# Crossing the second chunk of each pair over TensorE's array, and spreading the key products and turns through the inverse of an RWKV-7 recurrence

## The reference

```
def _wkv7_step(state, inp):
    r_t, w_t, k_t, v_t, a_t, b_t = inp
    sa = einsum('bhvk,bhk->bhv', state, a_t)
    state = state * w_t[:, :, None, :] + sa[..., None] * b_t[:, :, None, :] + v_t[..., None] * k_t[:, :, None, :]
    y = einsum('bhvk,bhk->bhv', state, r_t)
    return state, y
```

## Time and profile before

| | us |
|---|---|
| median of three runs | 2360.57 |
| the profiled execution | 2356.65 |
| its span | 2354.9 |
| the recurrence, from its first matmul to the first of the next stage | 897.69 to 1137.29 in the span |
| TensorE busy in the span | 2167.8 (92%) |
| VectorE busy in the span | 1294.9 (55%) |

### The profile page before, as it was taken

One profiled execution on the slowest core, in us unless ns is written; L12 is line 12 of the kernel. 1 busy time (PEld: TensorE's weight loads), 2 busy tenths in 40 slices (PEclk: granted clock), 3 DMA queues, 4 the chain that ended last, 5 costly groups with the idle time before them and its releaser, 6 DMA issues. The chain is left out here.

```text
span 2354.9 us, 36913 instructions
## 1 busy us (share of the span) xinstructions
PE 2167.8 (92%) x16050; PEld 1654.4 (70%) x16050; DVE 1294.9 (55%) x1837; ACT 768.9 (33%) x1111; POOL 281.4 (12%) x188
## 2 busy tenths in 40 slices
PE   7998989999979957999898999999976988999998
PEld 3885767887858617999455888887534665888885
DVE  2335756665454566555435766733386536766534
ACT  2434644443224430000224222322244624222322
POOL 0000003335400071111320000000004400000000
PEclk9998999999989968999979999999887999999999
DMA  6232002212213200000111233232320021333231
GB/s 270 96 99 82 1 10 84 69 56 80 95 60 99 83 0 3 4 4 4 32 33 56 90 99 99 90 99 80 104 69 1 1 63 54 99 99 99 90 99 45
DMA packets 46850, 158.81 MB, mean 67 GB/s; under 512 B 5232, under 2 KB 7280, under 8 KB 46688
## 3 DMA queue, kind: packets, MB, share of 16 engines
q1 hardware_dynamic: 44832, 150.84, 20.0%
q10 hardware_dynamic: 1856, 5.60, 0.7%
HBM read 154.28 MB, written 2.14 MB: 66 GB/s over the span
## 5 line engine op out<-in xcount | busy, mean ns | idle before, releaser
L923 PE MATMUL banks<-up_x_high,up_w_high 128*128 128x512 f32 x1056 | 412.3, 390 | 8.5 <-DVE up_w_low L917 3.9
L924 PE MATMUL banks<-up_x_low,up_w_high 128*128 128x512 f32 x1056 | 411.5, 390 | 0.0
L925 PE MATMUL banks<-up_x_high,up_w_low 128*128 128x512 f32 x1056 | 411.4, 390 | 0.0
L917 DVE TENSOR_TENSOR up_w_low<-weight_ring,up_w_high 128x1024 fp32r<-128x1024 f32 x132 | 161.6, 1226 | 272.1 <-ACT up_w_high L912 272.1
L912 ACT CAST up_w_high<-weight_ring 128x1024 fp32r<-128x1024 f32 x132 | 138.3, 1049 | 365.4 <-PE banks L925 340.8
L923 PEld LDWEIGHTS banks<-up_x_high,up_w_high 128*128 128x128 f32 x1056 | 198.5, 188 | 53.8 <-issue 11.7
L925 PEld LDWEIGHTS banks<-up_x_high,up_w_low 128*128 128x128 f32 x1056 | 198.6, 188 | 41.2
L924 PEld LDWEIGHTS banks<-up_x_low,up_w_high 128*128 128x128 f32 x1056 | 198.7, 188 | 41.0
L1443 POOL TENSOR_TENSOR hproj_w_low<-weight_ring,hproj_w_high 128x1024 fp32r<-128x1024 f32 x43 | 106.0, 2465 | 510.4 <-ACT hproj_w_high L1251 510.4
L976 DVE SCALAR_TENSOR_TENSOR act<-banks,cols,act 128x511 f32<-128x511 f32 (+1 forms) x176 | 131.9, 749 | 6.2
L1131 PE MATMUL banks<-hproj_x_high,hproj_w_high 128*128 128x512 f32 x224 | 90.1, 402 | 5.2 <-DVE hproj_x_low L1396 3.4
(11 more groups left out here) (453 smaller groups left out, 4391.3 us busy)
## 6 DMA issues: line engine op xcount, KB each, us to landing
weight_ring<-in_up SPq DMA_DIRECT2D x88, 512.0 KB, 3.6
weight_ring<-in_down SPq DMA_DIRECT2D x44, 512.0 KB, 3.6
weight_ring<-in_w_ada SPq DMA_DIRECT2D x24, 512.0 KB, 5.7
weight_ring<-in_w_rkv SPq DMA_DIRECT2D x24, 512.0 KB, 3.3
weight_ring<-in_w_in SPq DMA_DIRECT2D x20, 512.0 KB, 3.4
weight_ring<-in_w_out SPq DMA_DIRECT2D x16, 512.0 KB, 3.3
weight_ring<-in_w_q SPq DMA_DIRECT2D x8, 512.0 KB, 6.3
weight_ring<-in_w_k SPq DMA_DIRECT2D x8, 512.0 KB, 3.3
```

What stands on the lines that cost most here:

```text
L917: nc.vector.tensor_tensor(w_low[:, n % 2, :], ring[:, i % RING, :], w_high[:, n % 2, :].bitcast(f32), ALU.subtract).then_inc(wl_made, 1)
L923: nc.tensor.matmul(PS[:, bank, :], high, x_high[:, k, :], start=start, stop=False)
L924: nc.tensor.matmul(PS[:, bank, :], high, x_low[:, k, :], start=False, stop=False)
L925: return nc.tensor.matmul(PS[:, bank, :], low, x_high[:, k, :], start=False, stop=stop)
```

## The change

`SIDES` gives chunk x = 0 the same half in and out (`SAME`) and chunk x = 1 the other half out (`CROSS`), in `q_level`, in the product that adds to G, and in `make_w`. With this the second chunk's Q, GT and W lie with the two heads of each pair swapped, and its products of these kinds use the upper right and lower left corners. `q_level` and the product for G are written with the chunks alternating inside `p`, so that four products to four corners follow one another. The product for GT is written chunk by chunk, after that for G, and reads and writes one half. DVE takes both G before both GT. POOL's last step of the second chunk is cut in two, one for each half, so a pair has 7 operations there and not 6. The products of k and the turns leave `all_grams`: they follow half levels of the same pair (`fill`), the k products of the first chunk behind the first `q_level`, those of the second chunk in two parts, and one turn behind each half level from the fifth on. The banks move accordingly.

```
+                def key_gram(i, x, part):
+                    c = 2 * i + x
+                    if part == 0:
+                        pe.wait_ge(gram_moved, 6 * i + 3 + 2 * x)
+                    for p in range(4 * part, 4 * part + 4):
...
+                def fill(i, h):
+                    if h == 0:
+                        key_gram(i, 0, 0)
+                        key_gram(i, 0, 1)
+                    elif h in (2, 3):
+                        key_gram(i, 1, h - 2)
+                    elif h >= 4:
+                        turn(2 * i + (h - 4) // 3, (h - 4) % 3, (v, kt, bt)[(h - 4) % 3])
 
                 def q_level(i, l):
                     for x in range(2):
                         if l == 1:
-                            pe.wait_ge(start_made, 6 * i + 3 * x + 3)
-                            pe.wait_ge(gram_moved, 6 * i + 5 + x)
+                            pe.wait_ge(start_made, 7 * i + 1 + 3 * x)
+                            pe.wait_ge(gram_moved, 6 * i + 4)
                         else:
                             pe.wait_ge(g_moved, 8 * i + 2 * (l - 2) + x + 1)
...
+                    for p in range(8):
+                        for x in range(2):
+                            nt = with_b[(2 * i + x) % 4].rearrange("p (h w) -> p h w", h=8)
+                            for half, side in SIDES[x]:
+                                mm = nc.tensor.matmul(PS[side, x, pair_cols(p)], nt[half, p, 0:LC], G_[x][half, pair_cols(p)], start=True, stop=True)
...
                 def g_level(i, l):
                     for x in range(2):
                         pe.wait_ge(q_moved, 10 * i + 2 * (l - 1) + x + 1)
                         if l > 1:
                             pe.wait_ge(gt_moved, 10 * i + 2 * (l - 2) + x + 1)
+                    if l == 1:
+                        pe.wait_ge(start_made, 7 * i + 7)
+                    if l < LEVELS:
                         for p in range(8):
+                            for x in range(2):
+                                c = 2 * i + x
+                                for half, side in SIDES[x]:
+                                    mm = nc.tensor.matmul(PS[half, x, pair_cols(p)], GT_[c % 4][side, pair_cols(p)], Q_[x][side, pair_cols(p)], start=True, stop=True)
+                    for x in range(2):
+                        c = 2 * i + x
+                        for p in range(8):
+                            for half, side in SIDES[x]:
+                                mm = nc.tensor.matmul(PS[side, 2 + x, pair_cols(p)], Q_[x][side, pair_cols(p)], GT_[c % 4][side, pair_cols(p)], start=True, stop=True)
                         mm.then_inc(g_made, 1)
```

More of the change, by code:

```diff
@@ L1701, in program @@
         HALVES = (slice(0, HD), slice(HD, P))
+        SAME, CROSS = tuple(zip(HALVES, HALVES)), tuple(zip(HALVES, HALVES[::-1]))
+        SIDES = (SAME, CROSS)
         by_pair = lambda t: t.rearrange("p (h l) -> p h l", h=8)
@@ L1733, in turn @@
                         for half in HALVES:
-                            mm = nc.tensor.matmul(PS[half, 6 + i % 2, pair_cols(p)], of_head(t, p, half, c), ident64[half, :], start=True, stop=True)
+                            mm = nc.tensor.matmul(PS[half, 4 + i % 2, pair_cols(p)], of_head(t, p, half, c), ident64[half, :], start=True, stop=True)
                     mm.then_inc(turned, 1)
@@ L1744, in all_grams @@
                     gram(b, 2, bt, (at_, rt))
[L1745 to L1754, removed]
+                def key_gram(i, x, part):
[3 more added lines that the diff above has]
+                    for p in range(4 * part, 4 * part + 4):
+                        for j, right in enumerate((at_, rt)):
+                            at0 = 2 * p + j
+                            for half in HALVES:
+                                mm = nc.tensor.matmul(PS[half, 4 + at0 // 8, at0 % 8 * LC:(at0 % 8 + 1) * LC], of_head(kt, p, half, c), of_head(right, p, half, c), start=True, stop=True)
+                    if part == 1:
+                        mm.then_inc(grams, 1)
+                def fill(i, h):
[6 more added lines that the diff above has]
+                        turn(2 * i + (h - 4) // 3, (h - 4) % 3, (v, kt, bt)[(h - 4) % 3])
                 def q_level(i, l):
@@ L1765, in q_level @@
[L1765 to L1768, removed]
+                    for p in range(8):
[3 more added lines that the diff above has]
+                                mm = nc.tensor.matmul(PS[side, x, pair_cols(p)], nt[half, p, 0:LC], G_[x][half, pair_cols(p)], start=True, stop=True)
+                            if p == 7:
+                                mm.then_inc(q_made, 1)
@@ L1778, in g_level @@
+                    if l < LEVELS:
                         for p in range(8):
[L1779 to L1784, removed]
+                            for x in range(2):
+                                c = 2 * i + x
+                                for half, side in SIDES[x]:
+                                    mm = nc.tensor.matmul(PS[half, x, pair_cols(p)], GT_[c % 4][side, pair_cols(p)], Q_[x][side, pair_cols(p)], start=True, stop=True)
+                                if p == 7:
+                                    mm.then_inc(gn_made, 1)
@@ L1792, in make_w @@
                         pe.wait_ge(s_zero, 1)
-                    pe.wait_ge(turned_moved, min(6 * (c // 2 + 2), 24))
+                    pe.wait_ge(turned_moved, 6 * (c // 2 + 1))
                     ak = with_k[c % 4].rearrange("p (h w) -> p h w", h=8)
                     for p in range(8):
[L1796 to L1799, removed]
+                        for half, side in SIDES[c % 2]:
+                            nc.tensor.matmul(PS[side, 6, pair_cols(p)], of_head(at_, p, half, c), S_[half, pair_cols(p)], start=True, stop=False)
+                        for half, side in SIDES[c % 2]:
+                            mm = nc.tensor.matmul(PS[side, 6, pair_cols(p)], ak[half, p, 0:LC], of_head(v, p, half, c), start=False, stop=True)
                     mm.then_inc(w_made, 1)
@@ L1805, in make_u @@
                     for p in range(8):
-                        for half in HALVES:
-                            mm = nc.tensor.matmul(PS[half, 7, pair_cols(p)], GT_[c % 4][half, pair_cols(p)], W_[half, pair_cols(p)], start=True, stop=True)
+                        for half, side in SIDES[c % 2]:
+                            mm = nc.tensor.matmul(PS[half, 7, pair_cols(p)], GT_[c % 4][side, pair_cols(p)], W_[side, pair_cols(p)], start=True, stop=True)
                     mm.then_inc(u_made, 1)
@@ L1844, in _ @@
                         for part in range(2):
+                            step = 2 * (l - 1) + part
                             if i < NCH // 2:
                                 (g_level if part else q_level)(i, l)
-                            step = 2 * (l - 1) + part
+                                fill(i, step)
                             if i and step < 8:
@@ L1905, in _ @@
                     if i < NCH // 2:
-                        for n, x in enumerate((0, 0, 1, 1, 0, 1)):
+                        for n, x in enumerate((0, 0, 1, 1)):
                             take_gram(i, n, x)
@@ L1910, in _ @@
                             if i < NCH // 2:
-                                for x in range(2):
-                                    (take_g if part else take_q)(i, l, x)
+                                for take in (take_g, take_gt) if part else (take_q,):
+                                    for x in range(2):
+                                        take(i, l, x)
                             step = 2 * (l - 1) + part
+                            if i < NCH // 2 and step in (0, 3):
+                                take_gram(i, 4 + step // 3, step // 3)
                             if i and step < 8:
@@ L1940, in _ @@
                 for i in range(NCH // 2 + 1):
[L1941 to L1946, removed]
+                    for step in range(2 * LEVELS):
+                        if i < NCH // 2 and step >= 4:
+                            take_turned(2 * i + (step - 4) // 3, (step - 4) % 3)
+                        if i and step in (2, 6):
+                            take_y(2 * i - 2 + step // 4)
         checkpoint("wkv", ALL(r))
```

50 lines of the change are left out of this document (29 added, 21 removed).

## The result

The changed kernel is slower: a median of 2367.12 us against 2358.86 us of the kernel before in the same rounds (20 runs each), ratio 1.0032, 95% interval 1.0023 to 1.0042. Forecast were 2343 us, a range of 2334 to 2362 and a chance of 0.81 for faster.

What follows compares the result with a forecast made beforehand. TensorE's order of instructions was taken to bound the state recurrence stage. Terms: -33.6 + 10.5 + 1.0 + 4.2 + 4.0 - 6.9 + 3.4 = -17.4 us, giving 2343 us against the median; range 2334 to 2362.

Steps and rivals of the forecast that it cites:

- the sum of the other terms: State recurrence stage: all waits added and removed plus clock losses, without the four-corner saving; +16.2 us.
- the wait on POOL: Before `q_level` 1, behind the 96 grams: TensorE waits for POOL's fourth operation, four pairs, 10.5 us in all.
- half levels on DVE: Before `g_level`, TensorE waits while DVE masks both Q: 7 times 0.6 us, 4.2 us.
- grams on ACT: The grams of three pairs wait for ACT's last turned copy: 0.9 us each, 2.7 us.
- the last carry's turns: The first step of the last carry waits for its turns: 0.8 us.
- an assumed two: Clock falls behind the four new 2.5 to 2.7 us waits: two assumed, 1.7 us lost each, 3.4 us.
- the first pair's second wait on POOL: First pair's `g_level` 1 waits for POOL's three further operations: 1.0 us.
- I take the whole of it: 1152 matmuls of `q_level` and the product for G fall from 58.3 to 29.2 ns on four corners: -33.6 us.
- the issue floor: Rival, 6%: TensorE takes one small record in 22 ns, 44 ns a four-corner matmul; saving shrinks 17.0 us, 2360 us.
- the text's own point, 44 ns: Break-even: from 44 ns for a four-corner matmul on, the saving no longer pays the other 16.2 us.
- the pace also halves with the clock: Check on 64-column matmuls, 58.3 against 106 ns: issue at a fixed rate would not halve, so the array sets pace.
- two corners at a time: Rival, 9%: corners sharing rows or columns take turns, 58.3 ns a matmul stay; +16.2 us, 2377 us, slower.

Runs made afterwards that it cites:

- the two-corner run: Changed kernel with both chunks on the same side of the array (SAME for x = 0 and x = 1), all else as changed: 2377.46 us, ratio 1.0071.
- the wide products: Half level products at 128 moving columns, half as many: changed kernel 2336.83 us; same on two corners 2368.34 us; stages 30.3 us apart.
- half_before: Kernel before, every state recurrence product cut to 32 weight and 32 moving columns, same instructions: 2344.39 us, ratio 0.9934.
- pool_first: Changed kernel with GpSimd's two operations adding the identity to G moved first in each pair: 2362.86 us, ratio 1.0025.

## Why the prediction was wrong

**Right:** the array's speed in four corners, and the sum of the other terms. Without four corners that sum was +16.2 us; the two-corner run costs 17.1 in the stage and 0.71% in time, 17 us. Its parts: the wait on POOL 10.2 for 10.5; half levels on DVE 4.0 for 4.2; grams on ACT 2.3 for 2.7; the last carry's turns 0.8 for 0.8. The clock fell three times for an assumed two, 5.1 us for 3.4. Foreseen but absent: the first pair's second wait on POOL (1.0) and the turn behind DVE (0.5). That the sum comes so near is in part these misses cancelling the third fall of the clock.

**The step that failed:** "so two corners work at once, and the array, not the issue, sets the pace", and from it "I take the whole of it", -33.6. The first half holds: two corners at 64 columns are bound by the array. What does not follow is that the next limit is far off. Of the 33.6 us, 30 issue waits took 17.0 as recorded and, at 0.16 each for records that outlast their slots, some 4.8 more, and 9.4 us of saving are left by the two-corner run; the last 2.4 are not accounted for. So the term should have been -9.4: 16.2 - 9.4 = +6.8, and +8.5 with the measured 3 falls of the clock, against a measured +7.75 in the stage and +8.3 in the medians.

**The rival that was nearest** was the issue floor at 6%, and its mechanism was wrong too: it set a rate for each record, 22 ns. Records start 15 ns apart in a burst; it is the average over 256 instructions that is held, at 3.7 us. Its figure of a matmul, 44 ns, was too kind: 3.73 us for 64 is 58 ns, the very pace of before, and only the stretches behind a wait, when packets have come in ahead, run faster. By the text's own point, 44 ns, the change was bound to lose. The check "the pace also halves with the clock" was true of the array and said nothing of how near the second limit lay. The same rival with 25 ns for a record, the figure of the Trainium skill ("TensorE: Matmul & The Clock Gate", Back-to-back issue gap) that the prediction quotes, gave an estimated +6.7 us and 2367 us, which is the measured time. That is luck: a saving of 9.4 us over 1152 products does make 50 ns for each, but as an average of bursts at 30 ns and of waits for packets. No least distance of 25 ns holds here, where 64 records start within 0.94 us.

**The rival at 9%, two corners at a time,** said slower, and it was slower, but for another reason: the bursts at 30 ns and the 30.3 us of the wide products show all four corners at work, and its 2377 us is the time of the two-corner run (2377.46).

The trace of before held the number: its instruction queue moves 53 packets in 205 us of this stage, one in 3.87, while the array used one in 3.73 when it did not wait. Whether packets could come faster was not to be seen there, but a rival with the array's gain capped at that pace had a row behind it, and had a price: nearly the whole 33.6 us.

**Open:** what sets the 3.7 us (distances from 3.2 to 4.2 occur in `half_before`). A packet takes only some 1.1 us of its DMA engine (1.8% of 16 engines' 205 us for 52). The packet records show the rest in two parts: 2.2 to 2.9 us (median 2.5) from a packet's setting off to the end of the issue wait behind it, and 1.0 to 1.8 us (median 1.2) from there to the next packet's setting off, in all 47 cases of `half_before`, and alike in 29 of 30 in the changed kernel. In a stretch that waits for instructions the packets thus follow one after another and are never on their way together. What holds the next one back, and what fills the rest of the 2.5 us beside a transfer of 1.1, no run tried. How many packets lie ahead of TensorE is known only roughly: after the wait of 2.63 us at 910.60 the first issue wait comes 316 matmul records later, two and a half packets. A wait that is removed could therefore come back as issue waits, but in `pool_first` it did not: those fell from 17.0 to 14.7 us, and the saved 10.2 us on POOL came back as 5.6 on DVE and 4.8 on POOL. Why its median gained so little beside the 4.9 us of its profiled stage stays open.
